# Eight diagonals, tile 0's first inputs beside the last gathers, and another way to select an expert group's rows

## The reference, cut to what matters

```python
# first block, per layer: 128 (expert, gate) pairs for every token
a   = einsum('cd,ced->ce', h, u[expert])          # 128 rows of u per token, 1024 long
act = gelu(a) * gate
y   = einsum('ce,ced->cd', act, v[expert])        # 128 rows of v per token
# second block, per layer
proj = rms_norm(x, attn_norm[l]) @ w_in           # 1024 -> fq 512 | fk 512 | fv 512 | rest 424
...                                               # two causal attentions, w_o
group_id = argmax(softmax(x @ w_group))           # 8 groups of 4 experts, 2 experts per token
y[token] += gate * (silu(xb @ w_gate[e]) * (xb @ w_up[e])) @ w_down[e]
```

## Time and profile before

| | us |
|---|---|
| median of 3 runs | 2704.87 (2701.38 to 2715.58) |
| the profiled execution, its time | 2707.11 |
| its span | 2705.1 |
| busy in it: PE, DVE, ACT, POOL | 2179.8 (81%), 1349.8, 765.7, 1044.2 |
| gathers, first u gather to the last | 170.1 to 1813.3 |
| second block, layer 0: mixer, experts | 1829 to 2008, 2008 to 2262 |
| second block, layer 1: mixer, experts | 2264 to 2442, 2442 to 2696 |

### The profile page before, as it was taken

How to read it: one execution, slowest core, us unless ns; L and a number is a source line. 1 busy time by engine, 2 the same in 40 slices (tenths; PEclk the granted TensorE clock), 3 DMA queues, 4 the chain that set the end, 5 groups by cost and what they waited for, 6 DMA issues and landing times. The chain is left out here.

```text
span 2705.1 us, 27891 instructions
## 1 busy us (share of the span) xinstructions
PE 2179.8 (81%) x8660; PEld 1169.4 (43%) x8660; DVE 1349.8 (50%) x2888; ACT 765.7 (28%) x2242; POOL 1044.2 (39%) x1107
## 2 busy tenths in 40 slices
PE   4787877676877878878876667778889998989997
PEld 2455544222333343434533222225655554655554
DVE  6755577675466465574674764432522223332222
ACT  2243232232434334352332333332410002320001
POOL 4035555667666546665565666650010000000000
PEclk9899888888999989998988889889889999978999
DMA  9758888999999999999989999992159995218995
GB/s 369 286 197 309 303 325 334 392 375 405 409 413 410 404 357 381 401 378 345 355 321 349 400 373 366 368 362 94 47 209 413 410 406 204 78 52 354 409 405 239
DMA packets 236993, 879.67 MB, mean 325 GB/s; under 512 B 23283, under 2 KB 29955, under 8 KB 214339
## 3 DMA queue, kind: packets, MB, share of 16 engines
q0 software_dynamic: 149488, 543.97, 52.4%
q1 hardware_dynamic: 87380, 334.23, 31.5%
HBM read 877.07 MB, written 1.05 MB: 325 GB/s over the span
## 5 line engine op out<-in xcount | busy, mean ns | idle before, releaser
L1496 PE MATMUL PS<-arena 128*128 128x512 f32 x2048 | 1029.9, 653 | 330.6 <-issue 164.8
L2146 DVE CUSTOM_DVE_ANT_0 JK<-arena,PS 128x1024 bf16<-128x1024 f32 x512 | 624.9, 1220 | 499.3 <-DMA arena<-in_peer_u_dram,IDX 386.6
L1496 PEld LDWEIGHTS PS<-arena 128*128 128x128 f32 x2048 | 406.5, 208 | 913.1 <-issue 857.9
L905 POOL DMA_INDIRECT arena<-in_peer_v_dram,IDX x512 | 502.9, 982 | 468.7 <-PE PS L1496 249.1
L902 POOL DMA_INDIRECT arena<-in_peer_u_dram,IDX x512 | 496.4, 970 | 309.4 <-issue 145.3
L1048 ACT ACTIVATE ACTV<-DOT 128x1 f32<-128x1 f32 x512 | 101.4, 198 | 669.9 <-DVE DOT L2146 419.5
L1061 ACT ACTIVATE arena<-IDENT,GACT 128x128 f32<-128x128 f32 x512 | 205.5, 401 | 129.3 <-remote 63.6
L1860 PE MATMUL PS<-arena,HT 128*64 128x256 f32 x2048 | 237.5, 385 | 0.0
L1860 PEld LDWEIGHTS PS<-arena,HT 128*64 128x64 f32 x2048 | 142.4, 138 | 84.9 <-issue 20.7
L1056 ACT ACTIVATE GACT<-ACTV,GATE 128x1 f32<-128x1 f32 x512 | 150.8, 295 | 21.2 <-DVE GATE L2134 2.8
L1474 PE MATMUL PS<-HT,arena 128*128 128x128 f32 x896 | 123.8, 300 | 33.5 <-issue 32.6
(11 more groups left out here) (340 smaller groups left out, 1848.2 us busy)
## 6 DMA issues: line engine op xcount, KB each, us to landing
arena<-in_w_gate_dram SPq DMA_DIRECT2D x64, 1024.0 KB, 9.7
arena<-in_w_up_dram SPq DMA_DIRECT2D x64, 1024.0 KB, 11.9
arena<-in_w_down_dram SPq DMA_DIRECT2D x64, 1024.0 KB, 8.7
arena<-in_w_ada_dram SPq DMA_DIRECT2D x22, 2048.0 KB, 12.6
arena<-in_w_in_dram SPq DMA_DIRECT2D x11, 2048.0 KB, 14.4
arena<-in_peer_wq_dram SPq DMA_DIRECT2D x10, 2048.0 KB, 9.4
arena<-in_w_out_dram SPq DMA_DIRECT2D x6, 2048.0 KB, 11.8
arena<-in_peer_u_dram,IDX POOLq DMA_INDIRECT x512
```

The lines of the kernel that those rows point to most:

```text
L905: pool.indirect_dma_start(out=GV[b], out_offset=None, in_=v_rows, in_offset=off).then_inc(v_loaded[b], 16)
L1496: last = pe.matmul(PO[:, half, :], DIAG[:, n % DIAGS, :], GV[BUF[n]][:, half * 512:(half + 1) * 512], start=(j == 0), stop=False, skip_gro ...
L2146: dve.tensor_tensor_reduce(JUNK, GU[BUF[n]], HP[tt].rearrange("p b n -> p (b n)"), 1.0, 0.0, ALU.mult, ALU.add, DOT[:, s:s + 1]).then_inc( ...
```

## The change

It has three parts. **Eight diagonals.** DIAGS becomes 8. The four further ones take the place of JUNK and TMP in the tile JK: the dot's unread elementwise output is now f32 and goes over the u rows that it reads, the squares of the mixer's y rows go to another dead buffer, and the two helpers that used TMP use a part of HR or mod.

**Tile 0's first inputs.** Of the first mixer of the second block, tile 0's share of the norm, the transposes, `rest` and fq is put beside the last run of gathers, at slots 62 to 79; AN of layer 0 gets a place of its own. In both layers fq is computed by tile: HT stationary becomes HT streaming with 128 columns (`queries_of`, 32 matmuls per tile); fk stays with both tiles at once.

**The selection.** `pick` has SEL's 64 columns stationary and streams HR, 512 columns at a time, 4 matmuls; the selected rows are copied to XS, 4 transposes turn them (`turn_picked`), and one copy brings them to HTB. `slot_gates` stands before `gate_up`, and DVE's `select` before the copy of pass 3's `gate_up`.

```diff
-DIAGS = 4
+DIAGS = 8
@@ psum_jobs, last run of slots
+        if j == 68:
+            halves("bhT", 0, 0, BESIDE_TILE1)
+        if j == 71:
+            add(("rest", 0, 0), "v", BESIDE_TILE1)
+        if j == 76:
+            add(("fq", 0, 0), "s", BESIDE_TILE1)
@@ psum_jobs, second block
-        for tt in range(TT):
+        for tt in range(l == 0, TT):
             halves("bhT", l, tt)
             add(("rest", l, tt), "v")
-        for b in range(4):
-            add(("fqk", l, b), "s")
+        for tt in range(l == 0, TT):
+            add(("fq", l, tt), "s")
+        for b in range(2):
+            add(("fk", l, b), "s")
@@ places
-        DIAG = g3(8192, DIAGS, P)
+        DIAG = [tile[:, n * P:(n + 1) * P] for tile in (gv(8192, 512), JKT[:]) for n in range(DIAGS // 2)]
+        XS = mod[:, 9752:10264]
-        AN = mod[:, 2760:3784]
+        AN = [mod[:, 8984:10008], mod[:, 2760:3784]]
@@ ACT, last run of slots
+                if j == 64:
+                    x_root(0)
+                if j - 1 == 68:
+                    transposed("bhT", 0, 0)
+                if j - 1 == 76:
+                    queries_of(0, 0)
@@ ACT, experts
-                        for c in range(2):
-                            act.wait_ge(picked, 2 * i + (2 * l * NGB + c + 1))
-                            act.activation(HTB[:, c * 4:(c + 1) * 4].rearrange("p k t -> p (k t)"), PS[:, c, 0:4 * BT],
-                                           ACT.Copy).then_inc(picked_out, 1)
+                        act.wait_ge(picked, i + (l * NGB + 1))
+                        act.activation(XS, PS[:, 0, :], ACT.Copy).then_inc(picked_out, 1)
+                        act.wait_ge(rows_turned, i + (l * NGB + 1))
+                        act.activation(HTB.rearrange("p m c t -> p (m c t)"), PS[:, 1, :], ACT.Copy).then_inc(rows_turned_out, 1)
@@ PE, first inputs
+            def queries_of(l, tt):
+                loaded(pe, ("bin", l, 0))
+                w = ring[CH[("bin", l, 0)][1]].rearrange("p (k n) -> p k n", k=KT)
+                begin(("fq", l, tt))
+                for j in range(4):
+                    for k in range(KT):
+                        last = pe.matmul(bank(("fq", l, tt))[:, j * P:(j + 1) * P], w[:, k, j * P:(j + 1) * P],
+                                         HT[:, k, tt * P:(tt + 1) * P], start=(k == 0), stop=(k == KT - 1))
+                last.then_inc(psum_ready, 1)
@@ PE, last run of slots
+                if j == 68:
+                    turn_rows("bhT", 0, 0)
+                if j == 71:
+                    taken(pe, ("bhT", 0, 0, 1))
+                    rows_by(("rest", 0, 0), "bin", 0, 0, 3, REST, False)
+                if j == 76:
+                    queries_of(0, 0)
                 slot_add(1, 1, j)
@@ PE, experts
-                    for k in range(KT):
-                        for tt in range(TT):
-                            last = pe.matmul(PS[:, k // 4, (k % 4) * BT:(k % 4 + 1) * BT], HR[:, tt, k * P:(k + 1) * P],
-                                             SEL[:, tt, 0:BT], start=(tt == 0), stop=(tt == 1))
-                        if k % 4 == 3:
-                            last.then_inc(picked, 1)
+                    for tt in range(TT):
+                        for c in range(2):
+                            last = pe.matmul(PS[c * BT:(c + 1) * BT, 0, :], SEL[:, tt, 0:BT],
+                                             HR[:, tt, c * 512:(c + 1) * 512], start=(tt == 0), stop=(tt == 1))
+                    last.then_inc(picked, 1)
+
+                def turn_picked(i):
+                    pe.wait_ge(picked_out, i + (l * NGB + 1))
+                    for m in range(4):
+                        last = pe.transpose(PS[:, 1, m * P:(m + 1) * P], XS[:, m * P:(m + 1) * P], IDENT)
+                    last.then_inc(rows_turned, 1)
...
                         down(*before(i, s, 2))
+                    if s == 0:
+                        turn_picked(i)
                     if n:
                         turn(*before(i, s, 1))
+                    if s == 0 and n:
+                        slot_gates(i)
...
+                    if s == 0:
+                        pe.wait_ge(rows_turned_out, i + (l * NGB + 1))
@@ DVE, slot_dot
-                dve.tensor_tensor_reduce(JUNK, GU[BUF[n]], HP[tt].rearrange("p b n -> p (b n)"), 1.0, 0.0, ALU.mult, ALU.add,
+                dve.tensor_tensor_reduce(GU[BUF[n]], GU[BUF[n]], HP[tt].rearrange("p b n -> p (b n)"), 1.0, 0.0, ALU.mult, ALU.add,
                                          DOT[:, s:s + 1]).then_inc(dot_ready, 1)
@@ DVE, last run of slots
+                if j == 62:
+                    ask_root()
+                if j == 67:
+                    dve.wait_ge(params_loaded, pb + 16 * 11)
+                    gained(0, AN[0], rows_ready)
+                if j == 79:
+                    rest_copied(0, 0)
                 slot_dot(1, 1, j)
@@ DVE, experts
-                    dve.wait_ge(gate_up_done, b + 1)
-                    if s == 0:
-                        dve.wait_ge(slot_gates_out, i + (l * NGB + 1))
-                    dve.tensor_scalar(GUO[:, s % 2], ...).then_inc(gate_up_out, 1)
                     if s == EXP_RING - 1:
...
                         select(i + 1)
+                    dve.wait_ge(gate_up_done, b + 1)
+                    if s == 0:
+                        dve.wait_ge(slot_gates_out, i + (l * NGB + 1))
+                    dve.tensor_scalar(GUO[:, s % 2], ...).then_inc(gate_up_out, 1)
```

More of the change, by code:

```diff
@@ L874, in params_of_b @@
                     params([
[L875 removed]
+                        (AN[l], row(attn_norm_2[l], P)), (FN, row(ffn_norm_2[l], P)),
                         (BFB, row(b_f_2[l], P)), (QG, row(q_norm_2[l], P)), (KG, row(kv_norm_2[l], P)),
@@ L1246, in _ @@
                 low_rank_root()
-                for b in range(4):
-                    dst = (FQT, FKT)[b // 2]
-                    copy_out(("fqk", l, b), dst[:, 2 * (b % 2):2 * (b % 2) + 2, :],
-                             bank(("fqk", l, b)).rearrange("p (g t) -> p g t", g=2))
+                for tt in range(l == 0, TT):
+                    queries_of(l, tt)
+                for b in range(2):
+                    copy_out(("fk", l, b), FKT[:, 2 * b:2 * b + 2, :], bank(("fk", l, b)).rearrange("p (g t) -> p g t", g=2))
                 for tt in range(TT):
@@ L1495, in slot_add, with rows_by, queries_of @@
                 for half in range(2):
-                    last = pe.matmul(PO[:, half, :], DIAG[:, n % DIAGS, :], GV[BUF[n]][:, half * 512:(half + 1) * 512],
+                    last = pe.matmul(PO[:, half, :], DIAG[n % DIAGS], GV[BUF[n]][:, half * 512:(half + 1) * 512],
                                      start=(j == 0), stop=False, skip_group_check=True)
                 last.then_inc(expert_added, 1)
+            def rows_by(name, wname, l, tt, c, n, give_back):
+                loaded(pe, (wname, l, c))
+                w = ring[CH[(wname, l, c)][1]][:, 0:KT * n].rearrange("p (k n) -> p k n", k=KT)
+                begin(name)
+                for k in range(KT):
+                    last = pe.matmul(bank(name)[:, 0:n], HT[:, k, tt * P:(tt + 1) * P], w[:, k, :],
+                                     start=(k == 0), stop=(k == KT - 1))
+                last.then_inc(psum_ready, 1)
+                if give_back:
+                    arrived(pe, name)
+                    release()
+            def queries_of(l, tt):
+                loaded(pe, ("bin", l, 0))
+                w = ring[CH[("bin", l, 0)][1]].rearrange("p (k n) -> p k n", k=KT)
+                begin(("fq", l, tt))
+                for j in range(4):
+                    for k in range(KT):
+                        last = pe.matmul(bank(("fq", l, tt))[:, j * P:(j + 1) * P], w[:, k, j * P:(j + 1) * P],
+                                         HT[:, k, tt * P:(tt + 1) * P], start=(k == 0), stop=(k == KT - 1))
+                last.then_inc(psum_ready, 1)
             def slots_of_tile0(l):
@@ L1693, in _ @@
                     rows_by(("rest", l, tt), "bin", l, tt, 3, REST, tt == 1)
-                for c in range(2):
-                    for j in range(2):
-                        weights_first(("fqk", l, 2 * c + j), l, "bin", c, 2 * P * j, j == 0, j == 1)
-                    arrived(pe, ("fqk", l, 2 * c + 1))
-                    release()
+                for tt in range(l == 0, TT):
+                    queries_of(l, tt)
+                arrived(pe, ("fq", l, 1))
+                release()
+                for b in range(2):
+                    weights_first(("fk", l, b), l, "bin", 1, 2 * P * b, b == 0, b == 1)
+                arrived(pe, ("fk", l, 1))
+                release()
                 pe.wait_ge(cn_ready, 4 * (l + 1))
@@ L2186, in slots_of_tile0, with gained, rest_copied @@
                     slot_dot(l, 0, j)
+            pb = 16
+            def gained(tt, gain, inc):
+                have_root(tt, tt + 1)
```

(22 more changed lines are left out.)

47 lines of the change are left out of this document (18 added, 29 removed).

## The result

The changed kernel takes 2671.4 us (median of 4, 2664.9 to 2678.2), the kernel before 2705.6 beside it; the ratio is 0.9869 [0.9826, 0.9911]. In two later comparisons it was 0.9878 [0.9848, 0.9909] and 0.9887 [0.9848, 0.9925]. So it is faster by 1.1 to 1.3%, 31 to 34 us, where 41 were forecast; the measured time lies in the stated range of 2636 to 2691. The profiled execution has a span of 2676.4 us, 28.7 less than before.

A forecast was written before the change was run, and what follows sets the result against it. DMA was taken to bound the gathers, PE the mixer, and PE and loads nearly equally the experts. -14.9 + 0.4 + 0 - 26.9 = -41.4 us takes 2707.1 to 2665.7, median about 2663.5; range 2636 to 2691.

The forecast's parts named there:

- rival (d): Gathers: the in-place f32 write slows the dot, up to 26 us per 0.1 us; 2723 us at 1.45; chance 0.07.
- I take 4, nearest to the reading that the v buffer is what is missing: Gathers, eight diagonals: a gain of 4 us, between bounds of 0 and 52 us for the whole program.
- What it waited for last was a gathered v tile: Gathers, stall at 1752: PE, idle 6.80 us, waited last for a v tile, so POOL's wait for a buffer stays.
- Part 2, behind the gathers: Layer 0's mixer: removing tile 0's first inputs saves 8.04 us, and fq by tile 6.9; together -14.9 us.
- Bounds 0 and 20; I take 4: Last run of gathers: tile 0's inputs delay slot 76's addition and slot 84's v gather, costing 4 us.
- The sign given for the last u gather: End of the fourth run of gathers: the last u gather comes within 5 us of 1813.
- Rival (c): Last run of gathers: the block of `rest` and fq starves PE for 20 us and stalls gathers; 2695 us; chance 0.09.
- The 8.3 us by which PE lags behind the last load are used up: End of layer 0's experts: PE's lag behind the last load, 8.3 us (8.6 in layer 1), is gained.
- the loads' end: Experts: seven periods shorten by 0.83 us each, 5.8 us, if the dips are caused by waits for PE.
- The 0.8 added for the clock in group 0: First expert group: PE, waiting for loads, may get full clock later; +0.8 us per layer, bounds -0.3 and +3.
- rival (a): Experts: loads are at their limit, dips included; period stays 30.79 and only the lag is gained; 2675 us; chance 0.22.
- (e): Experts: without waits for PE the loads keep 431 GB/s, 29.2 us per group; 2653 us; chance 0.06.

The follow-up runs named there:

- e1: The changed kernel with DIAGS = 4 in place of 8; 2667.1 us, ratio 0.989 [0.9856, 0.9923] to the kernel before.
- c1: The changed kernel run again, unaltered, as its chip's yardstick; 2663.2 us against 2694.7 for the kernel before.
- e8: The changed kernel with w_down on its own semaphore, waited for by down only, and queued one expert later; 2641.9 us, ratio 0.9803 to the kernel before.
- c2: The changed kernel run once more, unaltered, as another chip's yardstick; 2664.3 us against 2695.9 for the kernel before.
- e4: The changed kernel with the old selection, but `select` still before the copy of pass 3's `gate_up`; 2565.8 us, kernel before 2585.8.
- e7: The changed kernel with tile 0's fq as rows, 8 matmuls of 512 columns, not turned back to columns; 2546.6 us, kernel before 2585.8.
- e2: The changed kernel with tile 0's first inputs back behind the gathers and fq with both tiles at once; 2665.8 us, ratio 0.991 to the kernel before.
- e9: The kernel of e8 with tile 0's fq in quarters before slots 76, 78, 80 and 82; 2642.8 us, ratio 0.9809 to the kernel before.

## Why the prediction was right, and where not

**Which way, and how much.** Right in sign and inside the range; the sum was 7 us too good against the medians (10 in the two later comparisons), and 12.6 against the profiled pair.

**Part 1.** The dot at 1.22 us came as forecast, which refutes rival (d). "I take 4, nearest to the reading that the v buffer is what is missing": that POOL's waits stay was right (29 and 29), and whether the gain is 0 or 4 can't be told (e1). One step of the reading was wrong. "What it waited for last was a gathered v tile": the v rows of slot 101 are recorded as landed by 1744.36, and PE went on at 1752.69, 0.14 us after ACT's diagonal of that slot, which had waited for `expert_added` (more on this in the last section).

**Part 2, behind the gathers.** -14.0 us up to cT (47.65 to 33.64 us from the first transposes to cT) for -14.9. Of the 0.9 missing, 0.7 lie between the start of `rest` of the tile left and the next step (8.94 us for 8.25), and 0.2 in fq (7.68 us from its start to fk's, where 14.36 - 6.9 = 7.46 were reckoned). The other 1.2 of the -12.8 in the table is between cT and the first pick (129.0 for 127.8 us), where the granted clock stands at half for 38.5 us in place of 34.8.

**Part 2, beside them.** "Bounds 0 and 20; I take 4": the mechanism was named (slot 76, then the v gather of slot 84), and the hold at slot 84 is anything from none to 9 us in one execution to the next. What it cost in the whole isn't shown. The profiled pair lacks 7.0 us in the gathers, but the first run of gathers alone, beside which nothing of parts 2 and 3 stands, differs by +7.3 there and by -5.2 in c1. The four runs took 1662.6, 1647.5 and 1638.3 us in three executions for 1655.6 in the one of the kernel before, so that the forecast of 0 lies among them is luck as much as reckoning. The sign given for the last u gather, within 5 us of 1813, was met in none: 1818.7, 1807.2 and 1795.5 (the end of the last run shifts with the three before it). Rival (c) had the block of 17 to 20 us right, in three of five executions, and its loss of 20 us wrong.

**Part 3.** PE's period of 28.44 was 28.03: `pick` to `down` took 8.44 for 8.78 us, of which `pick` (1.72 from its start to the next step, for 1.86) and gate-up (3.47 for 3.61) make most; both are followed by a step of the same form, 128*64. The loads were the next bound, as forecast, with 30.11 per group for 29.96. The two terms of the sum that were too large are these. "The 8.3 us by which PE lags behind the last load are used up": they are used up whole, since the last gate-up now starts 0.05 us after the last w_down has landed, but they were 6.8; 8.3 was reckoned from the GB/s of a window, and the landing comes later. And the loads' end, counted from the first pick, came 4.5 us earlier (233.98 to 229.51), where 5.8 were forecast. The 0.8 added for the clock in group 0 wasn't paid, since the loads set the end. So 6.8 + 4.5 = 11.3 us in place of 13.3 in layer 0, and by the same landings 7.4 + 5.0 = 12.4 in place of 13.6 in layer 1.

What the sum didn't have is that `gate_up` waits for all three matrices of its expert, and the last to land is a w_down that it doesn't use. e8 takes this wait away and has 11.3 to 13.4 us less in the experts. The dips were caused by waits for PE, and rival (a) is refuted by the same windows and by the period of 30.11 for 30.79; (e) is refuted too, since 429 GB/s in one window is paid back by 411 in the next.

The Trainium skill ("DMA: Bandwidth & Descriptors", "Where 436 GB/s comes from") has a ceiling of 435 GB/s. Here a period of 30.11 us for 12.58 MB is 418 GB/s, held for 90 us. That is 4% under it and 17% over the HBM limit that the same section gives.

## What to carry to other kernels

Where PE and the loads are nearly equal, look at the ring's waits before the matmuls: one semaphore for three transfers made PE wait for the one that it needed last, and telling them apart took 11 to 13 us more out of the experts, about half of the 23.6 that the whole third part had brought. Work that is put beside a running queue of gathers may be stretched to more than twice its time. As fewer and longer matmuls it was stretched far less often here, but neither that nor the quarters gave a gain in the total that can be told. And an engine that is freed from a wait gains nothing that shows while another waits for the same event.

## What the runs showed of the hardware

The same kernel differed from chip to chip far more than by this change: the kernel before took 2695 to 2706 us beside the result, c1 and c2, and 2585.8, in one execution, beside e4 to e7. Each of the three chips of the experiments was used in one comparison only, so the chip and the occasion aren't told apart. Nearly all of the difference is in gathers: the first run took 398 to 418 us (up to the next run's first gather) in the ten traces of those three comparisons, and 355 to 360 in e4 to e7, the third 408 to 417 and 371 to 376. The second took 432 to 439 in all, and the changed kernel's experts of layer 0 229.3 to 229.6 in c1, c2 and the first comparison and 229.6 in e7.

What differs between the two kinds of traces is the counter `expert_added`. At the stall of the earlier trace rows the additions of slots 97 to 100 end at 1738.3 to 1745.9 (ends are modelled), and the only increments that the trace has between 1730 and 1759 stand at 1752.06, 1752.12, 1752.18 and 1752.24; ACT's diagonal, POOL's gather and PE follow within 0.7 us. Such bursts of three or more increments, less than 0.15 us one from the next, occur 14 to 19 times in each of ten traces, in which 364 to 381 increments are recorded for 512 additions. In e4 to e7 513 are recorded, with no burst, no block of 64 records before slot 76 was stretched, and PE has no gap over 1 us beside the gathers that nothing recorded ends, of which the ten others have 46 to 67. That all of it goes together suggests one cause; what it is, and whether the increments come late or the additions end later than modelled, stays open.

The granted clock between cT and the first pick took different courses: in the same 10 us of e2 and c1 (the last three numbers are clock, DMA share and GB/s) it is full (2.4 GHz) and 0.63, a mean of full and half (1.2 GHz), and from cT to the first pick took 123.9 and 129.2 us, of which 27.7 and 38.4 at half clock. The two windows don't hold the same work, since e2 comes there at another time. e9 has the course of e2, with 123.9 us. In both the clock is full 3 us after the first pick, and their first group takes 26.1 us; in the others it is full after 9 us in layer 0, and the first group takes 28.1 to 28.4 with the same instructions. Where the loads bind, that is hidden: e2 has 229.2 us in layer 0 all the same.

```profile
1912.00:1922.00 10.00, 9.84 (x73) 8.93 (x72) 7.89 (x11) 8.57 (x27) 0.00 (x0) 1.00 0.00 0
```

```profile
1912.00:1922.00 10.00, 8.74 (x46) 8.40 (x46) 4.02 (x8) 5.33 (x18) 0.00 (x0) 0.63 0.00 0
```
